# Stick-breaking attention: a group's output is copied out of PSUM by VectorE between its scans instead of by ScalarE

## The reference, cut to what matters

```python
def sb_attend(q, q_pos, k, v, k_pos):
    z = jnp.einsum('bqhd,bkhd->bhqk', q, k, preferred_element_type=jnp.float32) * (SB_HEAD_DIM ** -0.5)
    mask = (k_pos[None, :] < q_pos[:, None])[None, None]
    log_keep = jnp.where(mask, jax.nn.log_sigmoid(-z), 0.0)
    suffix = lax.cumsum(log_keep, axis=3, reverse=True) - log_keep
    a = jnp.where(mask, jnp.exp(jax.nn.log_sigmoid(z) + suffix), 0.0)
    return jnp.einsum('bhqk,bkhd->bqhd', a.astype(v.dtype), v)
```

## Time and profile before

| what | value |
|---|---|
| median of 3 runs | 2764.31 us (2760.12 to 2768.33) |
| the profiled execution: time, span | 2768.86 us, 2765.2 us |
| granted TensorE clock over the span | 0.988 |
| busy over the span: PE, DVE, ACT, POOL | 96%, 63%, 42%, 26% |
| the stick-breaking attention stage | about 1660 to 1924 us of the span |

### The profile page before, as it was taken

How to read it: one execution, slowest core, us unless ns; L and a number is a source line. 1 busy time by engine, 2 the same in 40 slices (tenths; PEclk the granted TensorE clock), 3 DMA queues, 4 the chain that set the end, 5 groups by cost and what they waited for, 6 DMA issues and landing times. The chain is left out here.

```text
span 2765.2 us, 40402 instructions
## 1 busy us (share of the span) xinstructions
PE 2667.1 (96%) x14531; PEld 2236.8 (81%) x14531; DVE 1733.0 (63%) x2331; ACT 1156.7 (42%) x2260; POOL 732.0 (26%) x627
## 2 busy tenths in 40 slices
PE   7989998999999999999899999998999999999998
PEld 6878887788888878888798887776878888788886
DVE  5656666376555688888410008887485555788887
ACT  4334445343333333344322219998343333333433
POOL 3200001135544400000221116666045544300001
PEclk9999999999999999999999999999999999999999
DMA  4211122514444573533234437763324444654342
GB/s 150 86 61 46 46 79 89 184 60 153 137 137 144 170 256 125 162 122 118 80 128 151 155 102 194 172 173 121 111 95 145 137 137 145 235 181 164 127 154 100
DMA packets 285877, 368.81 MB, mean 133 GB/s; under 512 B 25984, under 2 KB 205696, under 8 KB 285696
## 3 DMA queue, kind: packets, MB, share of 16 engines
q1 hardware_dynamic: 285696, 366.42, 41.7%
HBM read 242.19 MB, written 124.16 MB: 132 GB/s over the span
## 5 line engine op out<-in xcount | busy, mean ns | idle before, releaser
L2342 DVE TENSOR_TENSOR x<-m_ps,x 128x1024 f32<-128x1024 f32 x224 | 273.3, 1220 | 91.9 <-PE m_ps L79 91.8
L2051 POOL TENSOR_TENSOR m_u<-m_u,m_u 128x512 f32<-128x512 f32 x128 | 179.6, 1414 | 349.0 <-DVE m_u L2185 344.0
L1998 POOL TENSOR_SCALAR m_stat<-m_stat 128x1 f32<-128x1 f32 x36 | 12.1, 335 | 831.6 <-ACT m_sqjunk L1942 667.2
L2173 DVE TENSOR_TENSOR m_z<-m_ps,m_part 128x512 f32<-128x512 f32 x96 | 66.3, 691 | 143.8 <-PE m_ps L79 143.5
L1800 ACT COPY m_part<-m_ps 128x512 f32<-128x512 f32 x96 | 56.4, 588 | 205.2 <-PE m_ps L79 205.2
L2161 DVE TENSOR_TENSOR m_up<-m_upr,m_up 128x512 fp32r<-128x512 f32 x128 | 87.9, 707 | 28.5 <-ACT m_up L1787 28.5
L3300 ACT ACTIVATE e_b<-e_ps 128x512 f32<-128x512 f32 (+3 forms) x192 | 95.9, 500 | 12.1 <-PE e_ps L3518 11.6
L1787 ACT CAST m_up<-m_upr 128x512 fp32r<-128x512 f32 x128 | 75.7, 615 | 57.9 <-PE m_ps L79 57.9
L3302 ACT ACTIVATE e_ps<-e_ps 128x512 f32<-128x512 f32 (+3 forms) x192 | 96.3, 501 | 0.0
L2031 POOL TENSOR_TENSOR m_uprS<-m_upr 128x512 f32<-128x512 f32 x62 | 94.6, 1526 | 5.0 <-DVE m_upS3l L2161 4.9
L3583 PE MATMUL e_ps<-ident,e_b 128*128 128x128 f32 x576 | 94.7, 274 | 0.7 <-POOL e_b L3398 0.6
(11 more groups left out here) (1192 smaller groups left out, 9185.8 us busy)
## 6 DMA issues: line engine op xcount, KB each, us to landing
scratch_u<-m_u SPq DMA_DIRECT2D x224, 256.0 KB, 2.1
m_ur<-scratch_u SPq DMA_DIRECT2D x208, 256.0 KB, 2.7
m_upr<-in_mlp_w_up SPq DMA_DIRECT2D x32, 1024.0 KB, 5.9
m_wr<-in_mlp_w_down SPq DMA_DIRECT2D x64, 512.0 KB, 6.6
scratch_x<-x SPq DMA_DIRECT2D x18, 512.0 KB, 2.6
x<-scratch_x SPq DMA_DIRECT2D x8, 1024.0 KB, 9.5
scratch_qr<-a_qrst SPq DMA_DIRECT2D x9, 512.0 KB, 3.4
a_x<-in_x_prompt SPq DMA_DIRECT2D x8, 512.0 KB, 5.0
```

Of the source, the lines that this page charges most:

```text
L2051: pool.tensor_tensor(u_st[out][:], u_st[a][:], u_st[b][:], op).then_inc(u_summed.sem, 1)
L2342: dve.tensor_tensor(out, bank[:, at:at + 2, :], out, ALU.add).then_inc(summed.sem, 1)
```

## The change

The copy of a group's accumulator moves from ScalarE to VectorE. VectorE issues it at its odd steps n = 4g+7, behind the scan of the first chunk and the copy of turned weights and ahead of the scan of the second chunk. The last group's copy stands behind all of VectorE's steps, ahead of the low parts of the weights. What is copied, the four SBUF tiles, the stores and TensorE's wait for `o_done` stay as they are.

```diff
@@ block.scalar
-            o_done.start(act)
...
-            def output(i, g):
-                pv_done.wait(act, S.GROUPS * i + g + 1)
-                o_out[g % 4].wait(act, 16 * (S.GROUPS // 4 * i + g // 4))
-                act.copy(o_st[g % 4][:], bank[:, 7, 0:GQ].rearrange(
-                    "p (s c) -> p s c", s=2)).then_inc(o_done.sem, 1)
...
-                if values_of is not None and values_of % 4 == 2:
-                    output(i, values_of // 4)
@@ block.vector
+            o_done.start(dve)
...
+            def output(g):
+                pv_done.wait(dve, g + 1)
+                o_out[g % 4].wait(dve, 16 * (g // 4))
+                dve.tensor_copy(o_st[g % 4][:], bank[:, 7, 0:GQ].rearrange(
+                    "p (s c) -> p s c", s=2)).then_inc(o_done.sem, 1)
...
                             scan(i, n + S.AHEAD, j)
                         if j == 0 and S.tasks(n)[1:] and S.tasks(n)[1][0] == "prompt":
                             transposed(i, n)
+                        if j == 0 and n % 4 == 3 and (i or n > 3):
+                            output(S.GROUPS * i + n // 4 - 1)
...
             bodies(dve, body)
+            output(S.GROUPS * BODIES - 1)
```

More of the change, by code:

```diff
@@ L3327, in transposed, with step @@
                 act.copy(turned_rows(n, task), turned_in(m, task)).then_inc(t_out[0].sem, 1)
-            def output(i, g):
-                pv_done.wait(act, S.GROUPS * i + g + 1)
-                o_out[g % 4].wait(act, 16 * (S.GROUPS // 4 * i + g // 4))
-                act.copy(o_st[g % 4][:], bank[:, 7, 0:GQ].rearrange(
-                    "p (s c) -> p s c", s=2)).then_inc(o_done.sem, 1)
-            def step(i, n, last, values_of=None):
+            def step(i, n, last):
                 for j in range(3):
@@ L3341, in step @@
                         transposed(i, n, j)
-                if values_of is not None and values_of % 4 == 2:
-                    output(i, values_of // 4)
             def body(i, last):
                 for n in range(S.STEPS):
-                    step(i, n + S.VALUES_LAG, last, n)
+                    step(i, n + S.VALUES_LAG, last)
                     k = n - (S.STEPS - 2 * S.VALUES_LAG)
```

## The result

The changed kernel takes 2793.08 us, median of 4 runs (2790.82 to 2800.8), against 2764.33 us (2760.12 to 2768.33). The ratio is 1.0107, 95% interval 1.0088 to 1.0126: it is slower, by 28.8 us. The forecast was 24.4 us more, a time of 2788.7 us in a range from 2778 to 2798.

What follows compares the result with a forecast made beforehand. TensorE was taken to set the attention stage's pace, ScalarE close behind. Stalls of 23.3 us plus 1.1 at the stage's end gave 24.4 us on the median 2764.31: 2788.7 us, range 2778 to 2798.

Steps and rivals of the forecast that it cites:

- The chain and its place: Before next `values`: scores, two sigmoids, scan, copy of turned weights, output; 2.38, 2.21, 3.07, 2.96 us in four hand-overs.
- That stalls add and nothing absorbs them: TensorE, 98% busy in the attention stage, stands still by the chain's excess at each hand-over; 23.3 us, counted in full.
- the kinds: Four repeating accumulator hand-overs, from groups 8, 9, 10, 11; stalls 0.34, 0.51, 1.32, 1.04 us, occurring 8, 8, 7, 7 times.
- the link's end: Chain's last part, behind VectorE's copy of turned weights: output 0.32 us, then 0.05 us until TensorE's weight load starts.
- ScalarE's lag: From the tall step's scores' end to the sigmoid's start: shrinks from 0.48, 0.31, 0.10, 0.20 to about 0.10 us.
- ScalarE's relief: 32 copies of 0.36 us leave ScalarE, about 11.5 us of work, worth only what TensorE waits for it.
- The stage's end: Both low parts of the weights on VectorE stand behind the last output; the attention stage ends 1.1 us later.
- VectorE keeps up in part: Rival: the two short stalls all but vanish and the long ones shrink; sum 15 us, 2779 us; chance 0.09.
- it gets faster: Rival: output reaches TensorE in time and ScalarE's relief shortens waits for turned weights; at best 2759 us; chance 0.03.
- nothing changes: Rival: stalls hold but the rest of the stage or a later DMA wait absorbs them; within 0.3%, 8.3 us; chance 0.04.
- The dearer case: Rival: without ScalarE's shorter lag 5.4 us more, slow low part 1.4 more, 2795 us; costlier copy 2797; chance 0.08.
- A sign of being wrong: Would count against the forecast: short waits for the copy, less body growth, or TensorE's clock falling in its pauses.

Runs made afterwards that it cites:

- e1: Changed kernel with VectorE's output copy issued ahead of the first chunk's scan of step 4g+11; 2766.95 us, ratio 0.9997 to the kernel before.
- e3: Kernel before the change, ScalarE keeping the output copy but issuing it one step later, behind both chunks' sigmoids; 2796.16 us, ratio 1.0105.
- e2: Changed kernel with the output copy between the first chunk's scan and the copy of turned weights; 2784.05 us, ratio 1.0058 to the kernel before.
- e4: Changed kernel with every output copied twice on VectorE, first into a tile nothing reads; 2810.21 us, ratio 1.0150 to the kernel before.
- e7: Changed kernel with the output copy one place later, behind the second chunk's scan too; 2852.61 us, ratio 1.033 to the kernel before.
- the second profile: The changed kernel run once more, unaltered, for another profile; 2802.86 us in that one run.
- e5: Changed kernel with the output copy ahead of the first scan at the third and fourth kinds of hand-over only; 2776.39 us, ratio 1.0040 to the kernel before.
- the last experiment: Kernel with output ahead of the scan, plus ScalarE's turn(4g+7) copy before third-kind sigmoids and last output on ScalarE; 2768.09 us, 1.0014 to the kernel before.

## Why the prediction was right

**The chain and its place.** Right, and shown: the loss goes when the copy moves ahead of the scan (e1), comes without VectorE when ScalarE's copy moves behind the same work (e3), and grows or shrinks by each link added or taken (e2, e4, e7).

**That stalls add and nothing absorbs them.** Right: 27.1 us of stalls. The rounds between them grew by at most 0.04 us each, 0.8 us in all in the second profile; and e5 shows the kinds to be independent. A body of eight groups grew by 7.5 us (groups 8 to 15) instead of 6.4. The waits for the copy came to 28.5 us, just over the 20 to 28 forecast, and the longest of the usual ones to 1.7 us and not 1.4: TensorE's whole pause also holds idle time that was there before.

**The sizes of the terms.** The forecast of 23.3 us for the stalls was 3.8 us short. The largest part is the link's end: output and release were to take 0.32 + 0.05 us behind the copy of turned weights, and took 0.44, for the copy lasts 0.414 instead of 0.399 and the first weight load follows 0.11 us behind it. That is 0.07 x 30, some 2.2 us. The 0.05 came from a row in which the load waited for ScalarE's copy of the turned weights, and not for the output; in e3 a ScalarE copy of the output is followed after 0.11 us too, and in the last experiment above a VectorE copy of turned weights after 0.05 (1789.66 to 1789.71). So the size doesn't go with the engine that made the copy. ScalarE's lag did not shrink to 0.10 us in every first-kind hand-over (0.21 in four of eight), and in four of the second kind the scan started 0.08 us later against its sigmoid: 0.8 us. Then I took the rows of groups 8 to 11 for all; those of groups 12 to 15 give 0.37, 0.54, 1.32 and 1.08, which is 0.4 us more in all. Group 29's hand-over, in which TensorE has no more scores to make, cost 0.92 where others of its kind cost 0.61, and group 2's 1.67 where others cost 1.39: 0.6 us. In both ScalarE's lag was 0.38 us and not 0.10; why, isn't shown. These sum to 4.0, against 3.8 missed.

**One reading of the earlier trace rows was wrong.** The prediction takes from it that the copy behind the waiting scan waits too. The row doesn't show that. The scan had waited and started before TensorE had the copy's data ready, at 1767.99:

```profile
1767.78 0.96 DVE L3454 TENSOR_TENSOR_SCAN e_r1long<-e_ps,e_zero 128x384 f32<-128x384 f32 x1 [0.17 <-ACT e_ps L3302]
```

```profile
1767.39 0.60 PE L3583 MATMUL e_ps<-ident,e_b 128*128 128x128 f32 x4
```

What bears out the order of the queue is the changed kernel, in which the output's data lay ready from 1765.79 to 1769.84 while VectorE stood idle for 1.17 us.

**ScalarE's relief.** Right that it is small; e1 shows that alone it is worth nothing that can be measured, and its only yield seen in the changed kernel was the shorter lag. ScalarE's busy time fell by some 6 us and not by 12 and VectorE's rose by 8 and not 13: rows that follow on each other overlap, so a copy adds less to the busy time than its length, and VectorE's second low part got 1.4 us shorter. The price of the chain didn't rest on that.

**The stage's end.** Forecast 1.1 us, measured 1.1: from group 29's hand-over to the end of the last copy it takes 12.37 us (1940.02 to 1952.39), against 11.27 (1912.88 to 1924.15). The second low part ran in 1.22 us with GpSimd through since 1948.20, against 2.65 in the earlier trace rows. By the Trainium skill's page "SBUF — State Buffer", section "Who interferes with whom", a VectorE instruction with two SBUF inputs contends with a GpSimd instruction that reads SBUF; these two times agree with it.

**The rivals.** That VectorE keeps up in part, that it gets faster, and that nothing changes are out by the stalls. The dearer case, without ScalarE's shorter lag, is out too: the lag did shrink to 0.10 us in most hand-overs. The time alone would not have told, for 2793.08 lies between the forecast of 2788.7 and that rival's 2795; the rows decide. The Trainium skill, page "Perfetto Trace Analysis", section "Optimizing Scalar/DVE Operations", says that if VectorE is saturated, moving some of its work to ScalarE may make sense. It doesn't speak of the way that was taken here, from a loaded ScalarE to VectorE, for which busy time would argue in the same manner. e1 makes that move with a harmless place in the queue and gains nothing: ScalarE is busy for 93% of the stage, but TensorE's loads still wait 5.2 us for its copies of turned weights, against 5.7 before.

**A sign of being wrong that came once.** The prediction names a fall of TensorE's clock in its pauses as such a sign. In the first profile of the changed kernel it fell behind the pause of 2.00 us, and that round was 1.57 us longer; the forecast had nothing for it. In the second profile it didn't fall, and the stage was 29.0 us longer all the same.

**The sum.** 27.1 of stalls, 0.8 between them and 1.1 at the end are 29.0 us, by which the stage is longer in the second profile (31.2 in the first), and the medians differ by 28.8. That these agree so closely is partly luck: the interval of the ratio spans some 24 to 35 us, and what lies outside the stage is 1.4 us longer in the first profile of the changed kernel than in that of the kernel before, and 5.7 in the second.

## What to carry to other kernels

When work moves to another engine, its price is set by what stands ahead of it in that engine's queue, and by the deadline of whoever waits for it; busy time says nothing on either. For each moved instruction write down when its data is ready, what it is queued behind, what that waits for, and when the result is needed. Here a place one instruction earlier in the same queue was the difference between 28.8 us and none that could be measured.

## What the runs showed of the hardware

TensorE's clock can fall behind pauses of 2 us, and need not. One and the same pause of 2.0 us was followed by a stretch at 0.52 in one profile of the changed kernel and at 1.00 in another; in the kernel with the output behind both scans, with pauses of 1.8 to 3.4 us, it fell in 9 of 29 rounds: 8 times behind the 14 pauses of 2.3 us and more of the third and fourth kind, once behind the 15 others, and not behind the longest. A round with a fall was 1.4 to 2.8 us longer. What decides it these runs don't show.

When the output copy is what the next `values` waits for last, the first weight load starts 0.11 to 0.12 us behind the copy's recorded end and its matmul 0.14 to 0.15, whether VectorE (30 hand-overs of the changed kernel) or ScalarE made it (the kernel with ScalarE's copy one step later). A load that waits for a copy of turned weights as the last started 0.05 us behind it in the earlier trace rows (ScalarE's copy) and in the last experiment (VectorE's). Why the two differ isn't shown.
